# Moving the 64-row sample tile forward, routing in six batches, and GpSimd's group loop in chunks

## The reference, cut to what matters

```python
mix = group-wise RMS norm of the four parts, times out_norm
x   = x + g1 * (mix @ w_out)
h2  = rms(x, norm_ffn) * (1 + sc2) + sh2
# router: argmax of 4 group logits, then the two best of the group's 8 experts
e_logits = h2 @ router_e_w + router_e_b;  g_logits = h2 @ router_g_w + router_g_b
gates = softmax(two best) * softmax(g_logits)[best group]
y   = x + g2 * sum over the two experts of gate * ((silu(h2 @ wg[e]) * (h2 @ wu[e])) @ wd[e])
```

## Time and profile before

| | |
|---|---|
| median of 3 runs | 2570.75 us (2566.36 to 2571.59) |
| the profiled execution | 2563.86 us, span 2562.1 us |
| mean granted clock of TensorE | 0.939 |
| TensorE matmul busy | 2291.0 us (89% of the span) |
| VectorE, ScalarE, GpSimd busy | 895.5, 595.1, 287.0 us |

### The profile page before, as it was taken

How to read it: one execution, slowest core, us unless ns; L and a number is a source line. 1 busy time by engine, 2 the same in 40 slices (tenths; PEclk the granted TensorE clock), 3 DMA queues, 4 the chain that set the end, 5 groups by cost and what they waited for, 6 DMA issues and landing times. The chain is left out here.

```text
span 2562.1 us, 27941 instructions
## 1 busy us (share of the span) xinstructions
PE 2291.0 (89%) x7615; PEld 1133.8 (44%) x7616; DVE 895.5 (35%) x2161; ACT 595.1 (23%) x1054; POOL 287.0 (11%) x460
## 2 busy tenths in 40 slices
PE   4698999999796898899999939999999999999993
PEld 1243555444453444455545414444444444444441
DVE  4546553026552333455466541211111111111211
ACT  3500011235541222334333211111111111111111
POOL 0001020100001000000002121111111111111111
PEclk8899999999897888799999959999999999999997
DMA  9224131422446344122246244675558788687962
GB/s 378 87 109 123 51 66 50 158 98 94 136 162 219 147 146 147 41 79 77 76 134 228 97 165 141 211 264 180 170 191 323 268 324 324 219 323 267 314 209 59
DMA packets 106526, 438.92 MB, mean 171 GB/s; under 512 B 14956, under 2 KB 53580, under 8 KB 85884
## 3 DMA queue, kind: packets, MB, share of 16 engines
q1 hardware_dynamic: 76160, 309.46, 32.4%
q0 software_dynamic: 26160, 113.16, 16.2%
q10 hardware_dynamic: 4112, 15.14, 1.5%
HBM read 356.39 MB, written 83.10 MB: 172 GB/s over the span
## 5 line engine op out<-in xcount | busy, mean ns | idle before, releaser
L2403 PE MATMUL bank<-arena 128*128 128x512 f32 x1120 | 492.4, 596 | 14.5 <-issue 14.5
L2098 PE MATMUL bank<-arena 128*128 128x512 f32 (+1 forms) x960 | 359.4, 534 | 19.5 <-ACTq L1003 19.5
L2403 PEld LDWEIGHTS bank<-arena 128*128 128x128 f32 x1120 | 212.4, 190 | 290.5 <-issue 290.5
L2319 PE MATMUL bank<-arena 128*128 128x512 f32 (+1 forms) x544 | 262.9, 619 | 0.2 <-DMA arena<-mix_d 0.2
L2098 PEld LDWEIGHTS bank<-arena 128*128 128x128 f32 x960 | 168.6, 192 | 206.4 <-issue 185.2
L2431 PE MATMUL bank<-arena 128*128 128x512 f32 x560 | 250.3, 600 | 10.0 <-issue 10.0
L1988 DVE COPY arena<-bank 128x512 f32<-128x512 f32 x50 | 34.6, 693 | 550.0 <-PE bank L2418 550.0
L2431 PEld LDWEIGHTS bank<-arena 128*128 128x128 f32 x560 | 103.7, 190 | 133.8 <-issue 130.7
L2319 PEld LDWEIGHTS bank<-arena 128*128 128x128 f32 (+1 forms) x544 | 97.1, 193 | 92.1 <-issue 91.1
L2250 PE MATMUL bank<-arena 128*128 128x64 f32 x568 | 95.9, 302 | 35.2 <-ACTq L1160 21.9
L1998 DVE TENSOR_TENSOR arena<-bank,arena 128x512 f32<-128x512 f32 (+1 forms) x50 | 34.5, 690 | 255.8 <-PE bank L2431 209.3
(11 more groups left out here) (461 smaller groups left out, 2697.4 us busy)
## 6 DMA issues: line engine op xcount, KB each, us to landing
arena<-wg SPq DMA_DIRECT2D x32, 2048.0 KB
arena<-wu SPq DMA_DIRECT2D x32, 2048.0 KB, 15.1
arena<-wd SPq DMA_DIRECT2D x32, 2048.0 KB, 8.2
arena<-mod_w SPq DMA_DIRECT2D x12, 2048.0 KB, 13.0
z_d<-arena ACTq DMA_DIRECT2D x12, 1056.0 KB, 6.4
arena<-z_d POOLq DMA_DIRECT2D x10, 1056.0 KB, 7.5
arena<-kc POOLq DMA_DIRECT2D x8, 1280.0 KB, 6.0
arena<-vc POOLq DMA_DIRECT2D x8, 1280.0 KB, 5.6
```

Of the source, the lines that this page charges most:

```text
L2098: ins = mm(bank[n % 2][:, 0:w], wz[:, i % 3, k, :], hT[:, k, t0:t0 + w], start=(k == 0), stop=(k == KT - 1))
L2319: ins = mm(bank[5 + q][0:r], l, wo[:, k, 512 * q:512 * q + 512], start=(k == 0), stop=(k == KT - 1))
L2403: ins = mm(bank[bk][:, :], xgT[:, s, k, :], m[w][:, k, :], start=(k == 0), stop=(k == KT - 1))
```

## The change

The tiles are worked through in ORDER: 0 to 11, then the sample tile 16, then 12 to 15. So a step's i is now a place and no more a tile, and row numbers, attention reads and semaphore counts are taken from ORDER[i]. Routing has six batches, of 4, 4, 4, 1, 2 and 2 places. Batch 2 stays in rows 13-14; batch 3 (the sample tile) follows in rows 14-15, batch 4 in rows 16-17, and batch 5 runs whole in row 18. `rinit` writes the token numbers column by column. GpSimd's loop is split into chunks of four groups: a chunk's first group is tested, and if it isn't used the whole chunk is passed over. The other engines' loops stay as they are.

```diff
+        SAMPLES = 12
+        ORDER = [*range(SAMPLES), NT - 1, *range(SAMPLES, NT - 1)]
+        BATCHES = (range(0, 4), range(4, 8), range(8, 12), range(12, 13), range(13, 15), range(15, 17))
         RSTEPS = ["r0", "r1", "r2", "re", "rk", "r3", "r4", "sc"]
         ROUTE = {}
-        for b, i in ((0, 8), (1, 10), (2, 13), (3, 17)):
-            for j, names in ((2, RSTEPS[:1]), (4, RSTEPS[1:2]), (6, RSTEPS[2:4])):
-                ROUTE.setdefault((i, j), []).extend((f, b) for f in names)
-            for j, names in ((0, RSTEPS[4:6]), (2, RSTEPS[6:])):
-                ROUTE.setdefault((i + (b < 3), j if b < 3 else 7), []).extend((f, b) for f in names)
-        ROUTE.setdefault((NT + 1, 2), []).extend([("w1",)] + [(f, 4) for f in RSTEPS] + [("ut",)])
+        for b, at in enumerate((((8, 2), (8, 4), (8, 6), (9, 0), (9, 2)), ((10, 2), (10, 4), (10, 6), (11, 0), (11, 2)),
+                                ((13, 2), (13, 4), (13, 6), (14, 0), (14, 2)), ((14, 3), (14, 5), (14, 7), (15, 2), (15, 4)),
+                                ((16, 2), (16, 4), (16, 6), (17, 2), (17, 4)))):
+            for where, names in zip(at, (RSTEPS[:1], RSTEPS[1:2], RSTEPS[2:4], RSTEPS[4:6], RSTEPS[6:])):
+                ROUTE.setdefault(where, []).extend((f, b) for f in names)
+        ROUTE.setdefault((NT + 1, 2), []).extend([("w1",)] + [(f, 5) for f in RSTEPS] + [("ut",)])
...
         def batch(b):
-            return range(4 * b, min(4 * b + 4, NT))
+            return BATCHES[b]
+
+        def merged(i):
+            return i + 1 - (i > SAMPLES)
...
             def row_att(step, i):
-                t0 = i * P
+                t0 = ORDER[i] * P
                 if i >= 2:
                     sp.wait_ge(S("mrg_o"), i - 1)
-                if i < NT - 1:
+                if i != SAMPLES:
                     for q in range(2):
-                        sp.wait_ge(S(f"st_att{q}"), 64 * (i // 4 + 1))
+                        sp.wait_ge(S(f"st_att{q}"), 64 * (ORDER[i] // 4 + 1))
                     sp.dma_start(ma[:, i % 2].rearrange("p q h c -> p q (h c)"),
                                  att_d[:, t0:t0 + P].rearrange("q t c -> t q c")).then_inc(S(f"ld_ma{i % 2}"), 16)
...
                 for w in range(2):
                     for k in range(2):
-                        link(pool.iota(pay[:, :, k, w], pattern=[[P, NT]], base=0, channel_multiplier=1))
-                for k in range(2):
-                    link(pool.iota(pay[:, NT - 1:NT, k, 1], pattern=[[0, 1]], base=T + P, channel_multiplier=1))
+                        for i in range(NT):
+                            link(pool.iota(pay[:, i:i + 1, k, w], pattern=[[0, 1]], base=T + P if w and i == SAMPLES else ORDER[i] * P, channel_multiplier=1))
...
-                groups(pool, body)
+                body(0)
+                for first in range(1, LAST, 4):
+                    with pool.If(entry(pool, used, first * 2) > 0):
+                        body(first)
+                        with pool.Fori(first + 1, min(first + 4, LAST)) as it:
+                            with pool.If(entry(pool, used, it * 2) > 0):
+                                body(it)
+                with pool.If(entry(pool, used, LAST * 2) > 0):
+                    body(LAST)
...
             def mrg_exp(step, i):
-                if i < NT - 1:
-                    act.wait_ge(S("mrg_d"), i + 1)
+                if i != SAMPLES:
+                    act.wait_ge(S("mrg_d"), merged(i))
...
             def mrg_max(step, i):
-                if i == NT - 1:
+                if i == SAMPLES:
                     return
-                dve.wait_ge(S(f"ld_ma{i % 2}"), 16 * (i // 2 + 1))
+                dve.wait_ge(S(f"ld_ma{i % 2}"), 16 * sum(1 for p in range(i % 2, i + 1, 2) if p != SAMPLES))
...
             def prj_gate(step, i, q):
-                r = rows(i)
-                g = grow_s if i == NT - 1 else grow
+                r = rows(ORDER[i])
+                g = grow_s if i == SAMPLES else grow
...
             def route_group(step, b):
-                n, i0 = len(batch(b)), 4 * b
+                n, i0 = len(batch(b)), batch(b)[0]
...
-                if b == 4:
-                    link(dve.memset(lg[64:128, NT - 1], 0.0))
+                if SAMPLES in batch(b):
+                    link(dve.memset(lg[64:128, SAMPLES], 0.0))
...
-                w = 3 if b == 4 else 2
+                w = 3 if SAMPLES in batch(b) else 2
...
             def prj(step, i, q, part):
-                r = rows(i)
+                r = rows(ORDER[i])
```

More of the change, by code:

```diff
@@ L636, in row_in @@
             def row_in(step, i):
-                r, t0 = rows(i), i * P
+                r, t0 = rows(ORDER[i]), ORDER[i] * P
                 if i >= 2:
@@ L1783, in mrg_sum @@
                     dve.wait_ge(S("b7_full"), B7["mo", i - 2] + 1)
-                if i < NT - 1:
+                if i != SAMPLES:
                     m = ma[:, i % 2]
                     e1, e2, den, w1, w2 = (mw[:, n] for n in (4, 5, 6, 7, 8))
-                    dve.wait_ge(S("mrg_e"), i + 1)
+                    dve.wait_ge(S("mrg_e"), merged(i))
                     link(TT(w1, e1, m[:, 0, :, 65], ALU.mult))
@@ L1830, in x1_var @@
             def x1_var(step, i):
-                ss = mw[0:rows(i), 10, 0:1]
+                ss = mw[0:rows(ORDER[i]), 10, 0:1]
                 dve.wait_ge(S("x1_ss"), i + 1)
```

## The result

The changed kernel takes 2573.13 us (median of 20 runs, 2564.19 to 2580.78), that of before 2566.78 (20 runs, 2559.89 to 2571.86). The ratio is 1.0022, with a 95% interval of 1.0012 to 1.0032: 5.7 us slower (3.1 to 8.2). I had forecast 4.3 us less. The profiled execution of after took 2567.89 us, span 2566.1, granted clock 0.940.

The account below looks back on a forecast made before the run. TensorE bounds the row and expert stages, a chain of small steps follows the last projection, and GpSimd bounds the end. End -5.3 plus routing, taken as +1.0, gave -4.3: 2566.4 us from a 2570.75 median, range 2559 to 2573.

Parts of the forecast that it names:

- the tail: Chain from the last gate (1482.5) to the last scatter: last batch starts about 1496.1, takes 10.7, last scatter starts 1511.4.
- Constants: GpSimd's 62 more instructions add 12 us before VectorE first reads a constant, all covered: cost 0.
- rival 4: Sample tile's eight small reads delay SP behind expert weights, TensorE stands in row 11: +5 to +15; 0.08 with other losses.
- Batch of one in rows 14 and 15: TensorE in row 15: first product 0.8 late, stall and handover 3.9, rank products 0.9; taken as 5.5, bounds 2 and 8.
- rival 3: More stall in row 15, by a clock fall after the wait or VectorE's extra merge: +2 to +4 over the sum; chance 0.10.
- Sample tile at place 12: Places 12 and 16 only swap on TensorE; the merge moves from row 11 to row 15: cost 0.
- Table load before the root: ScalarE, left on the Exp table by the batch of two, reloads before tile 16's root: +1.28 on the chain.
- GpSimd's chunks: At the end, three tests replace eight, so the last add's landing at 2539.75 becomes the limit: -5.3 us.
- Rival 1: GpSimd's jumps over unused chunks at the end wait for code, 1.6 to 4.8; 0 to 3.5 of gain lost; chance 0.11.
- 10.8 behind: Profile sign at the end: the sums' read starts within 1 us of the last add's landing, not 10.8 behind.
- VectorE just in time: At the end, VectorE's unused rounds end at 2544.3 and the sums arrive at 2545.0, so VectorE does not limit.
- Expert stage: Stage between routing and end: TensorE's, not touched except in GpSimd's loop, where the tests' cost is hidden; put at nothing.

Follow-up runs that it names:

- the tile last: The changed kernel with GpSimd's plain loop and the sample tile left as the last row tile; ratio 1.0009 to the kernel before.
- The chunks alone: The kernel before with only GpSimd's loop by chunks of four groups, tiles and batches as before; ratio 0.9982, measured -4.6 us.
- after +11: The changed kernel with eleven more instructions (waits long fulfilled) in TensorE's stream ahead of the expert stage; ratio 1.0008 to the kernel before.
- +9: The kernel before with nine more instructions (waits long fulfilled) in TensorE's stream ahead of the expert stage; ratio 1.0019, 4.9 us slower.
- routing only: The changed kernel with GpSimd's plain loop again, keeping the moved sample tile and six batches; ratio 1.0033, +8.5 us against the kernel before.
- bounded loop: The kernel before with GpSimd's group loop bounded by a register holding the number of groups in use; ratio 0.9984, -4.1 us.

## Why the prediction was wrong, point by point

Three steps of the sum failed: the tail, where I priced turns and logits of a 128-row tile at 64 rows (2.5 us), GpSimd's jumps over unused chunks, which I priced as plain tests (1.9 us at the read), and the expert stage, which I put at nothing (2.5 us by the traces). Each turned a gain or a draw towards a loss.

- **Constants, 0.** Right: the 68 iotas end at 1288.7, their 13.31 us are hidden.
- **Eight sample reads (rival 4).** They took 11.13 us together, and nothing waited for them.
- **Batch of one in rows 14 and 15, +5.5.** The place and the stall were right; that the total came out was luck. From the start of row 15 to that of row 16 it is 23.02 against 17.40, 5.6 more. The stall is 3.49 where I had 3.7: against the first scatter ScalarE's copy ended 0.6 later than the sum said, and TensorE got there 1.0 later. The two rank products took 0.44 and not 0.9, and the late first product 0.4 (in row 14) and not 0.8. The 1.7 that make up for it are the clock's fall behind the stall, a term that the sum hadn't; I had it as a bound of this part and in rival 3, with a chance of 0.10.
- **Sample tile at place 12, 0.** Wrong: the places don't just swap. Row 12 took 18.00 and not 17.08, row 13 0.2 more, and row 16 gave back only 0.5 (row 14's 0.4 comes with the batch, since it is there with the tile last too). The merge that row 15 has now comes on ScalarE ahead of the copy that the ranks wait for (its root at 1451.55, the copy at 1451.86), and with the tile last the same batch stalls 1.08 and not 3.49. Rival 3 had this merge too.
- **Table load before the root, 1.28.** Right.
- **The tail.** The step of the routing sum that failed. I made a copy wider (0.38 to 0.6) and kept the turns and the logits of the 64-row tile, "1.93". With 128 rows at the 1.2 GHz level they took 3.60, and the turns 0.43 more each: 2.5 us on a chain where nothing overlaps. Last gate to last batch took 16.4, not 13.6. The batch itself took 10.6 for 10.7, the scatters kept their 1.27. With 1.2 more from the rows and 0.5 less for the last landing, the routing part was +4.4 to the read of the table, +3.8 to the first add, and not +1.1.
- **GpSimd's chunks, -5.3.** Three tests, as forecast, but the read of the sums came 9.18 after the last add and not 7.3 (2540.63 less 2533.35 in my sum): gain 3.4, 2.95 with the landing of the read (4.82 for 4.39). Rival 1 is what happened at this place, at the price that I had put on it from the earlier trace rows, and I gave it 0.11. The chunks alone, with one gap, came near my number (7.78 for the read, time -4.6). The "10.8 behind" in what I said the profile would show was misread: it is GpSimd's idle time ahead of the read, and the read started 6.1 behind the landing. The rule of the Trainium skill (Runtime: NRT & Kernel Launch, Instruction fetch mechanics), that a taken branch outside of the loaded blocks waits for a fetch, speaks for these gaps; that they are fetches is argued, not shown. It rests on the packets in that window and on the absence of gaps and packets in a loop that jumps over no code. That there is one gap in one kernel and two in another (1.55 and 2.58 in after +11) says that their number and length depend on where GpSimd's code lies. "VectorE just in time" was right, and it is why a loop without the gaps isn't faster until VectorE's is bounded too.
- **Expert stage, 0.** A term that I had put at nothing without a reason ("is not touched"): no step of mine costed what nine more instructions of TensorE ahead of a loop do to it. By the time of +9 it is 4.9 us (2.1 to 7.7), by after with eleven more 3.6. The traces show 2.5, of which 2.1 to 2.4 are the eight stalls; whether there is more is open.

The sum then: routing +3.8, end -3.0, and the place of TensorE's code +2.5 by the traces or +3.6 to 4.9 by the times: 3.3, or 4.4 to 5.7, for 5.7 measured (3.1 to 8.2). One point stays open. The eight stalls are no loads of code: they all lie between 1650 and 2530, and there the DMA view has two instruction packets in before and two in TensorE +9, whose stalls are long (six in after). In the stall shown above the sequencer of after loses 0.18 at the branch at the head of the loop and 0.17 at a table read, and is level elsewhere; that of +9 loses 0.14 and 0.17 at the same two places, that of after +11 nothing there. What in the engine depends on the place of the code there, I haven't found.

## What to carry to other kernels

When a smaller piece of work is moved forward, cost what stands at the end in its place: every operation on the last chain at the larger size and at the clock of that stretch. When a stall of TensorE is priced, ask what its clock does behind it: here that was half as much again. When code is put ahead of a hot loop, or a loop is unrolled into chunks, look at the stalls of each engine's sequencer after it: nine instructions of TensorE made eight stalls about a seventh longer, and eleven idle ones took that back. To skip unused rounds, bound the loop by a register and do so on every engine that the end waits for; copies of the body trade tests for gaps.

## What the runs showed of the hardware

- TensorE's eight stalls are 1.80 to 2.29 us long with its stream as before (15.8 together), and 2.03 to 2.53 in the five kernels with nine instructions more ahead of them (17.8 to 18.2); with five or twenty more the sum is as before.
- An unused round of GpSimd's plain loop took mostly 1.21 us before and 1.02 in routing only, whose GpSimd stream is longer ahead of it.
- After a wait of 3.49 us between full stretches TensorE's granted clock fell to 0.50 for a while (0.71 over 5.8 us), and twelve products took 7.09 us and not 5.42. It did so in all three traces with that wait, and in row 15 of no other.
- Two jumps of GpSimd over unused code took 2.08 and 2.26 us, with instruction packets in flight; in the chunks alone one took 2.84 and the other nothing that shows.
- At a granted clock of 0.50, sixteen logits products took 3.60 us with 128 rows and 1.93 with 64; at 1.00, 1.87 with 128 rows.
- The clock's dips (0.94 over one window of 30 us) cost 1.7 to 2.0 us each and come and go between executions of like kernels; the times of one kernel's runs go with their mean clock (bounded loop: 2556.72 at 0.942, 2568.66 at 0.937).
